# Projections of pool-conv and sparse attention as three fp32r products, attention outputs stored as halves

## The reference

```python
# second block, layer 0: pool-conv
proj = rms_norm(x, g) @ ab_w_in                    # 1024 x 1536: u_pool, u_val, u_gate
y = concat([pool_mixer(u_pool), conv_module(u_val, u_gate)]) @ ab_w_out   # 1024 x 1024
x = x + y
# second block, layer 1: sparse attention, 16 heads of 64
q, k, v, qi, ki, wi = split(rms_norm(x, g) @ c_w_in)
score = sum_h relu(qi_h . ki) * wi_h * scale       # 8 index heads; causal
sel = top_64(score)                                # keys kept for each query
x = x + softmax(q . k[sel] * 64**-0.5 + t5_bias) @ v[sel] @ c_w_out
# third block (twice): SwiGLU, then the hybrid mixer, then SwiGLU, each with a layer norm
y_ssm = mamba2(z, xbc, dt) @ w_ssm_out
y_att = moba_attention(q, k, v) @ w_att_out        # 8 heads of 128, one causal block of 256 keys
h = layer_norm(ALPHA * h + (g_ssm * y_ssm + g_att * y_att) @ w_o)
```

## Time and profile before

| | before |
|---|---|
| device time, median of 3 runs | 3935.52 us (3928.43 to 3944.9) |
| the profiled execution | 3925.62 us |
| its span | 3923.8 us |
| mean granted TensorE clock | 0.95 |
| TensorE busy | 3254.8 us (83%) |
| TensorE weight loads | 2228.5 us (57%) |
| VectorE busy | 2155.1 us (55%) |
| ScalarE busy | 1013.5 us (26%) |
| GpSimd busy | 1030.0 us (26%) |

### The profile page before, as it was taken

The page is one execution under the profiler, slowest core; times in us unless marked ns, Lnnn a source line. Parts: engine busy times, 40 slices in busy tenths (PEclk is TensorE's granted clock), DMA queues, the critical chain, the costliest instruction groups (busy, mean ns, idle before and its releaser), DMA issues. The chain is left out here.

```text
span 3923.8 us, 34661 instructions
## 1 busy us (share of the span) xinstructions
PE 3254.8 (83%) x12288; PEld 2228.5 (57%) x12288; DVE 2155.1 (55%) x3737; ACT 1013.5 (26%) x1593; POOL 1030.0 (26%) x1090
## 2 busy tenths in 40 slices
PE   5897577778987577777998999999998989978798
PEld 3663222223654222223877687876687868867686
DVE  5567766654547766654644445433455435555654
ACT  0212111111112111111432343411343422434333
POOL 0026777764015777775000000000000000200000
PEclk9799899999889899999999999999999989989999
DMA  9369999998539999998551455542355534243453
GB/s 364 142 260 385 409 409 409 409 399 328 212 123 380 409 409 409 409 409 326 172 185 65 140 185 168 189 150 97 119 192 166 190 130 143 76 157 122 150 183 118
DMA packets 402040, 951.18 MB, mean 242 GB/s; under 512 B 30652, under 2 KB 171488, under 8 KB 401632
## 3 DMA queue, kind: packets, MB, share of 16 engines
q0 software_dynamic: 147456, 536.94, 34.6%
q1 hardware_dynamic: 245088, 397.09, 29.7%
q10 hardware_dynamic: 9344, 15.22, 1.1%
HBM read 948.06 MB, written 1.07 MB: 242 GB/s over the span
## 5 line engine op out<-in xcount | busy, mean ns | idle before, releaser
L1451 PE MATMUL PS<-v_rows,xn 128*128 128x512 f32 x1944 | 910.0, 611 | 372.6 <-DMA v_rows<-in_peer_v_dram,peer_ids 369.7
L1451 PEld LDWEIGHTS PS<-v_rows,xn 128*128 128x128 f32 x1944 | 355.1, 193 | 926.4 <-issue 586.0
L1526 DVE CUSTOM_DVE_ANT_0 u_rows<-u_rows,PS 128x1024 f32<-128x1024 f32 x512 | 622.0, 1221 | 359.1 <-DMA u_rows<-in_peer_u_dram,peer_ids 331.4
L758 DVE TENSOR_TENSOR ring_lo<-ring,ring_hi 128x2048 fp32r<-128x2048 f32 x198 | 452.9, 2292 | 260.3 <-ACT ring_hi L697 259.8
L1590 POOL DMA_INDIRECT u_rows<-in_peer_u_dram,peer_ids x512 | 484.4, 946 | 282.2 <-issue 144.1
L1590 POOL DMA_INDIRECT v_rows<-in_peer_v_dram,peer_ids x512 | 486.0, 949 | 168.3 <-issue 143.0
L697 ACT CAST ring_hi<-ring 128x2048 fp32r<-128x2048 f32 x198 | 376.7, 1912 | 286.2 <-PE PS L614 156.2
L614 PE MATMUL PS<-ring_hi,hT_hi 128*128 128x512 f32 x1056 | 420.7, 398 | 16.6 <-DVE hT_lo L798 12.0
L614 PE MATMUL PS<-ring_hi,hT_lo 128*128 128x512 f32 x1056 | 414.8, 393 | 0.0
L614 PE MATMUL PS<-ring_lo,hT_hi 128*128 128x512 f32 x1056 | 414.0, 392 | 0.0
L440 PE MATMUL PS<-hT,ring 128*128 128x256 f32 x1664 | 364.0, 380 | 1.2 <-DVE hT L404 1.2
(11 more groups left out here) (395 smaller groups left out, 3714.4 us busy)
## 6 DMA issues: line engine op xcount, KB each, us to landing
ring<-in_ffn_w_gate_dram SPq DMA_DIRECT2D x132, 512.0 KB, 3.7
ring<-in_ffn_w_up_dram SPq DMA_DIRECT2D x132, 512.0 KB, 4.7
ring<-in_ffn_w_down_dram SPq DMA_DIRECT2D x66, 1024.0 KB, 4.9
ring<-in_w_in_dram SPq DMA_DIRECT2D x64, 1024.0 KB, 5.0
ada_ring<-in_ada_w_dram SPq DMA_DIRECT2D x96, 512.0 KB, 8.3
ring<-in_peer_wq_dram SPq DMA_DIRECT2D x16, 1024.0 KB, 5.4
ring<-in_c_w_in_dram SPq DMA_DIRECT2D x14, 1024.0 KB, 4.9
ring<-in_w_out_dram SPq DMA_DIRECT2D x8, 1024.0 KB, 11.4
```

The source lines that it names most:

```text
L758: nc.vector.tensor_tensor(halves(c)[1], slot, halves(c)[0], ALU.subtract).then_inc(S.w_lo, 1)
L1451: ins = nc.tensor.matmul(self.PS[:, 2 * b + h, :], diag[:, r % NDIAG, :], rowsV[:, m % VRING, h * BANK:(h + 1) * BANK], start=(n % (slots ...
L1526: ins = nc.vector.tensor_tensor_reduce(rowsU[:, m % URING, :], rowsU[:, m % URING, :], H[b], 1.0, 0.0, ALU.mult, ALU.add, dots[:, e:e + 1])
```

## The change

- `project_halves` makes every F product as three fp32r products of 256 columns (hi·hi, hi·lo, lo·hi), all into the same columns of a pair of banks; the four banks and the additions at emptying go. The T form is as it was, but in pairs of banks.
- `ab_in`, `ab_out`, `c_in` and `c_out` use it instead of `project`. Two helpers split the transposed tokens in two pieces each (`tokens_hi` on ScalarE, `tokens_lo` on VectorE). Chunks 2 and 3 of `c_in` (the index keys and weights) stay in plain fp32 and are left out of the halves (`plain`).
- `between` is called ahead of the wait for the root: VectorE makes the lo half of chunk 0 there.
- The pool and convolution stage makes the halves of its output and of the first chunks of `ab_out`.
- In both attentions the output leaves PSUM as two halves: ScalarE casts hi after the transposed probabilities of a later head, VectorE subtracts hi from the same PSUM tile. The split of all tokens in `att_out` goes.
- In `ssm_z` and `att_in` the queries and keys are emptied by ScalarE alone.

```diff
     def norm_vector(...):
+        if between:
+            between()
         ve.wait_ge(S.n_rstd, 1)
         for b in range(NB):
             nc.vector.tensor_scalar(self.xn[:, b, :], self.X[:, b, :], self.rstd[:, b:b + 1], None,
                                     ALU.mult).then_inc(S.n_xn, 1)
-        if between:
-            between()
...
+    def tokens_hi(self, act, S, hh):
+        act.drain()
+        for g in range(2):
+            if g == 1:
+                act.wait_ge(S.n_hT, self.N_HT)
+            self.nc.scalar.copy(hh[:, 4 * g:4 * g + 4, 0, :], self.hT[:, 4 * g:4 * g + 4, :]).then_inc(S.h_hi, 1)
+
+    def tokens_lo(self, ve, S, hh):
+        ve.drain()
+        for g in range(2):
+            ve.wait_ge(S.h_hi, g + 1)
+            self.nc.vector.tensor_tensor(hh[:, 4 * g:4 * g + 4, 1, :], self.hT[:, 4 * g:4 * g + 4, :], hh[:, 4 * g:4 * g + 4, 0, :],
+                                         ALU.subtract).then_inc(S.h_lo, 1)
...
     # project_halves, kind "F"
-                            out, col = self.PS[:, quad + t, :], slice(t * P, (t + 1) * P)
-                            nc.tensor.matmul(out, w_hi[:, kk, col], both[:, k, :], start=st, stop=False, skip_group_check=True)
-                            ins = nc.tensor.matmul(out[:, 0:SEQ], w_lo[:, kk, col], tok_hi[:, k, :], start=False, stop=sp,
-                                                   skip_group_check=True)
+                            out, col = self.PS[:, pair + t // 2, (t % 2) * SEQ:(t % 2 + 1) * SEQ], slice(t * P, (t + 1) * P)
+                            nc.tensor.matmul(out, w_hi[:, kk, col], tok_hi[:, k, :], start=(st and t % 2 == 0), stop=False, skip_group_check=True)
+                            nc.tensor.matmul(out, w_hi[:, kk, col], tok_lo[:, k, :], start=False, stop=False, skip_group_check=True)
+                            ins = nc.tensor.matmul(out, w_lo[:, kk, col], tok_hi[:, k, :], start=False, stop=sp, skip_group_check=True)
...
     # ab_in: TensorE, ScalarE, VectorE
-                    self.project(pe, S, [("F", 512)] * 3, self.hT, KT)
+                    self.project_halves(pe, S, ["F"] * 3, hh[:, :, 0, :], hh[:, :, 1, :], KT, ready=S.h_lo)
...
+                    self.weights_hi(act, S, 0, 2)
                     self.norm_scalar(act, S, gain, None)
+                    self.tokens_hi(act, S, hh)
+                    self.weights_hi(act, S, 2, 6)
...
+                    self.norm_vector(ve, S, gain, None, lambda: self.weights_lo(ve, S, 0, 1))
+                    self.tokens_lo(ve, S, hh)
+                    self.weights_lo(ve, S, 1, 2)
...
     # pool and convolution stage: ScalarE, then VectorE
+                    self.weights_hi(act, S, 0, 2)
+                    act.wait_ge(S.y_pool, 1)
+                    nc.scalar.copy(YT_hi[:, 0:4, :], YT[:, 0:4, :]).then_inc(S.y_hi, 1)
...
                         nc.scalar.activation(YT[:, 4 + c, :], conv[:, c, :], ACT.Silu, bias=b[:, c:c + 1], scale=g[:, c:c + 1])
+                    for c in (0, 2):
+                        if c == 0:
+                            nc.scalar.drain()
+                        nc.scalar.copy(YT_hi[:, 4 + c:6 + c, :], YT[:, 4 + c:6 + c, :]).then_inc(S.y_hi, 1)
...
                     nc.vector.tensor_tensor(sq[:], conv[:], conv[:], ALU.mult).then_inc(S.sq, 1)
+                    self.weights_lo(ve, S, 0, 1)
...
+                    for i, c in enumerate((slice(0, 4), slice(4, 6), slice(6, 8))):
+                        ve.wait_ge(S.y_hi, i + 1)
+                        nc.vector.tensor_tensor(YT_lo[:, c, :], YT[:, c, :], YT_hi[:, c, :], ALU.subtract)
+                        if i == 0:
+                            self.weights_lo(ve, S, 1, 2)
...
     # output_projection (ahead: chunks whose halves an earlier stage made)
-                self.project(pe, S, [("T", 512)] * 2, YT, KT)
+                self.project_halves(pe, S, ["T"] * 2, YT_hi, YT_lo, KT)
+                self.weights_hi(act, S, self.ahead, 4)
+                self.weights_lo(ve, S, self.ahead, 4)
...
     # attention
+            def out_lo(h):
+                ve.wait_ge(S.a_hi, h + 1)
+                nc.vector.tensor_tensor(YT_lo[rows(h), h // per, :], self.PS[rows(h), 4 + h % 2, 0:SEQ], YT_hi[rows(h), h // per, :],
+                                        ALU.subtract).then_inc(S.a_out, 1)
...
                 normalised(h)
                 if h >= 2:
-                    self.attention_out(ve, S, nc.vector.tensor_copy, h - 2, rows, per, YT)
+                    out_lo(h - 2)
...
+            def out_hi(h):
+                act.wait_ge(S.a_val, h + 1)
+                nc.scalar.copy(YT_hi[rows(h), h // per, :], self.PS[rows(h), 4 + h % 2, 0:SEQ]).then_inc(S.a_hi, 1)
...
                 turned(h)
+                if h >= 2:
+                    out_hi(h - 2)
+            for h in (heads - 2, heads - 1):
+                out_hi(h)
...
     # c_in: ScalarE
+                    self.weights_hi(act, S, 4, 8)
                     for h in range(8):
                         act.wait_ge(S.index, h + 1)
...
                     for j in (3, 5, 7):
+                        self.weights_hi(act, S, 2 * j + 2, 2 * j + 6 if j < 7 else 2 * j + 3)
...
     # c_in: VectorE
+                    self.weights_lo(ve, S, 4, 6)
                     self.leave(ve, 1)
...
+                    self.weights_lo(ve, S, 6, 8)
                     evacuate(2)
...
                         nc.vector.drain().then_inc(S.used, 1)
+                    self.weights_lo(ve, S, 8, 10)
...
     # att_out
-                    if i == 0:
-                        nc.scalar.copy(YT_hi[:], YT[:]).then_inc(S.y_hi, 1)
...
-                    if i == 0:
-                        ve.wait_ge(S.y_hi, 1)
-                        nc.vector.tensor_tensor(YT_lo[:], YT[:], YT_hi[:], ALU.subtract).then_inc(S.y_lo, 1)
```

More of the change, by code:

```diff
@@ L478, in project_halves @@
                 if n >= self.base + self.ahead:
-                    pe.wait_ge(S.w_lo, n - self.base - self.ahead + 1)
+                    pe.wait_ge(S.w_lo, self.halves_made(n))
+                if ready is not None and j == first:
+                    pe.wait_ge(ready, g + 1)
                 w_hi, w_lo = [ring[:, n % self.half_slots, :].rearrange("p (k n) -> p k n", k=4)
@@ L1784, in _, with output_projection, attention @@
                     nc.gpsimd.tensor_tensor(self.rstd[:], self.ms[:], self.neghalf[:, 0:NB], ALU.pow).then_inc(S.c_rstd, 1)
-            self.output_projection("ab_out", YT)
-    def output_projection(self, name, YT):
-        with self.stage("p_free0 p_free1", name) as (block, S):
+            self.output_projection("ab_out", YT_hi, YT_lo, 2)
+    def output_projection(self, name, YT_hi, YT_lo, ahead):
+        self.ahead = ahead
+        with self.stage("p_free0 p_free1 w_hi w_lo", name) as (block, S):
             @block.tensor
             def _(pe):
-                self.project(pe, S, [("T", 512)] * 2, YT, KT)
+                self.project_halves(pe, S, ["T"] * 2, YT_hi, YT_lo, KT)
+            @block.scalar
+            def _(act):
+                self.weights_hi(act, S, self.ahead, 4)
             @block.vector
             def _(ve):
+                self.weights_lo(ve, S, self.ahead, 4)
                 self.plain_residual(ve, S)
-    def attention(self, block, S, ctx, heads, dh, QT, KT_, V, mask, bias, YT):
+    def attention(self, block, S, ctx, heads, dh, QT, KT_, V, mask, bias, YT_hi, YT_lo):
         nc = self.nc
@@ L1938, in sparse_attention @@
             gain = self.col("mix_norm_2")[:, KT:2 * KT]
-            with self.stage("n_ms n_rstd n_xn n_tr n_hT p_free0 p_free1 rb rb_out index relu used", "c_in") as (block, S):
-                rel = self.sb("dsa_rel", [P, 2, W3], ctx=ctx)
-                sc = self.sb("dsa_scores", [P, W3], ctx=ctx)
-                top = self.sb("dsa_top", [P, NB, 8], ctx=ctx)
+            self.place_halves(ctx, 2)
+            self.plain = (2, 3)
+            with ExitStack() as inner, self.stage(
+                    "n_ms n_rstd n_xn n_tr n_hT p_free0 p_free1 w_hi w_lo h_hi h_lo rb rb_out index relu used", "c_in") as (block, S):
+                rel = self.sb("dsa_rel", [P, 2, W3], ctx=inner)
+                sc = self.sb("dsa_scores", [P, W3], ctx=inner)
+                top = self.sb("dsa_top", [P, NB, 8], ctx=inner)
+                hh = self.sb("dsa_tokens", [P, KT, 2, SEQ], F32R, ctx=inner)
+                halves = hh[:, :, 0, :], hh[:, :, 1, :], KT
                 @block.tensor
@@ L2070, in _ @@
                     pe.wait_ge(side, 48)
-                self.attention(block, S, ctx, AH, 64, QT, KT_, V, mask[:], B, YT)
-            self.output_projection("c_out", YT)
+                self.attention(block, S, ctx, AH, 64, QT, KT_, V, mask[:], B, YT_hi, YT_lo)
+            self.output_projection("c_out", YT_hi, YT_lo, 1)
     def turn_plain(self, pe, S, src):
@@ L2635, in _ @@
                 nc.vector.drain()
[L2636 to L2640 removed]
+                self.plain_residual(ve, S)
```

138 lines of the change are left out of this document (69 added, 69 removed).

## The result

The changed kernel takes 3953.45 us (median of 20 runs, 3939.52 to 3964.95), the kernel before 3937.98 us (20 runs, 3923.86 to 3944.9). The ratio is 1.0053, with a 95% interval of 1.0042 to 1.0065: 20.9 us slower by the ratio, between 16.5 and 25.6, and 15.5 by the two medians. The forecast was 3940 us, in a range of 3918 to 3960. One thing in the text ahead is wrong and changes no number: the third block runs once, not twice.

What follows compares the result with a forecast made beforehand. TensorE was taken as gapless in fp32 projections; in the attention loops VectorE and TensorE both repeat every 2.82 us. Stage terms summed to +0.1, the clock added +4: 3935.5 + 4.1 = 3940 us, range 3918 to 3960.

Steps and rivals of the forecast that it cites:

- clock term: Whole kernel: new waits make TensorE start at 1.2 GHz, about 2 us each; half of four starts, +4 us.
- rival (2): Attention loops: waits pull the clock down, making the loop TensorE-bound again; all 14 heads give 3960 us; chance 0.12.
- Products: Converted projections: three 256-wide fp32r products cost 0.348 us against 0.434 for fp32; three 512-wide ones 0.677 against 0.86.
- Rival (3): Projections: 256-wide products are bound by their weight loads, 0.57 us a triple, +85 us, 4025 us; chance 0.03.
- Loops: Both attention loops: VectorE waits for ScalarE's hi half, period 4.0 us; +16.5 us in sparse attention, +7.6 in the second.
- Rival (1): Attention loops: the hi-half wait isn't on the path, so 24.1 us go away, 3916 us; chance 0.09.
- The two stalls ahead of jobs 5 and 7: Sparse attention's input: ScalarE empties jobs 3 and 5 only after the fourth hi half; TensorE stands 3.1 us twice, +6.2.
- Start of `ab_in` and end of pool-conv: Pool-conv: first input product starts 2.95 us later; VectorE's extra halves at the end add 2.8 us.
- `c_out`: Sparse attention's output projection: cheaper 512-wide products save 5.8 us.
- Rival (4): Converted stages: ScalarE and VectorE make halves late at most chunks, 6 to 10 us in all, 3948 us; chance 0.11.
- `c_in`: Sparse attention's input stage: cheaper products against a later start, a longer index phase and two stalls, together -7.5 us.
- The removed split in `att_out`: Third block's output projection: dropping the split of all tokens in one piece removes TensorE's 2.26 us wait, -2.3 us.

Runs made afterwards that it cites:

- experiment 1: Changed kernel with ScalarE's hi cast of head h-2 moved ahead of the copy of head h's transposed probabilities; ratio to the kernel before 0.9979.
- experiment 3: Changed kernel with ScalarE, in the sparse input stage, emptying jobs 3 and 5 after the second hi half, not the fourth; ratio to the kernel before 1.0018.
- the repaired loop: Sparse attention's loop with the hi cast ahead of the transposed probabilities' copy, against the changed kernel's order; 50.2 to 58.7 us in six traces.
- The kernel with all repairs: Changed kernel plus earlier hi cast, both sparse-input reorderings, pool-conv's end over its output projection, chunk 0's lo half behind the scaling; 0.9877 and 0.9910 of the kernel before.

## Why the prediction held, and which step of it failed

**The range and the sign.** The measured 3953.45 us lie in 3918 to 3960. The forecast was no change to speak of, +4 us. By the ratio the change costs 20.9 us, just beyond the half per cent (0.53), a case that had a chance of 0.16; by the medians it is 15.5, within it. The mechanisms of the loops and the waits were right. That the range held is in part luck: its clock term was to lie between 0 and 8 us and came out at some 19, and the range reached 20 us above the forecast for the sake of rival (2), which came only in part.

**Products: right.** Forecast 0.348 us a triple, measured 0.354 and 0.360; over the 256 triples that replace fp32 products that is 2 us less gain. The 512-wide triples of `c_in` take 0.700 us, not 0.677, which is 0.7 more; those of `c_out` came out at 0.680. Rival (3) fell: with a load for each product the spacing is 0.12, and not the 0.19 of a load. The rule of the Trainium skill that was weighed ("TensorE: Matmul & The Clock Gate", Part 3, what overlaps and what doesn't: loads overlap running products only when their row groups differ) is not what this trace shows, where all loads use all rows.

**Loops: right.** Forecast were a period of 4.0 us, 16.5 and 7.6 us more; measured 3.9 and 4.2 in turn, and against the first trace before 12 to 21 us and 9 to 9.6 us more (five traces). The chain was the one that was written down, instruction by instruction, and experiment 1 takes it away with a change of order alone. Rival (1) fell with that.

**The two stalls ahead of jobs 5 and 7: right**, 3.03 us for a forecast of 3.1. The index phase went to 9.2 us (2618.16 to 2627.32), forecast 8.3.

**Start of `ab_in` and end of pool-conv: right**, +3.15 for +2.95 (from the end of the last SwiGLU product to the first of `ab_in`, 2054.50 to 2065.20 before, 2047.93 to 2061.78 after) and +2.45 for +2.8 (TensorE's wait ahead of `ab_out`, 3.72 and 6.17). **`c_out`: right**, -5.7 for -5.8 in the first trace; in the second, where the clock was low at its start, -3.5. Rival (4) fell: no wait for `weights_lo` stands in a steady run of a stage that the change converts.

**The step that failed: the clock.** "I count half of four such starts: +4. The cost lies between 0 and 8." Against the same products at the full clock, the low clock costs the first trace 2.8 us in `ab_in`, 1.0 more than before in `ab_out`, some 6 in `c_in`, 1.7 in `att_out` and 2.9 in `mix3_out`. The loops are 2.8 and 2.0 us over their forecast, which counted none; that this is the clock as well is inferred, not measured apart. Together that is 19 us, in the second trace several less (`mix3_out` 1.6 less, the sparse loop 5.1). `c_in` shows it best: forecast -7.5, measured +2.4, though the start and both stalls came out to 0.2 us. Of the 9.9 us that were missed some 6 are the clock, 1.7 the price of the triples and 0.9 the index phase; the rest is not accounted for. The four starts that the prediction counted are the first products of two stages, the index phase and the second attention's loop, at half a start each. The two stalls that it had itself priced at 3.1 us each were not among them, and behind each the clock was low: experiment 3 got back 3.6 us of clock with the two. TensorE behind the wait ahead of job 5, and in the second attention's loop, which answers to the last of the earlier trace rows:

```profile
2654.00:2658.00 4.00, 3.08 (x14) 3.08 (x15) 3.93 (x5) 0.87 (x2) 0.00 (x0) 0.63 0.58 222
...
3592.00:3627.00 35.00, 24.12 (x88) 19.01 (x88) 17.70 (x56) 14.75 (x49) 0.00 (x0) 0.65 0.00 0
```

The loop's mean clock went from 0.82 to 0.65. In this stage idle time and low clock came together: the low clock is part of the price of the wait.

**Rival (2)** came in part. In the first trace the clock fell again in the middle of the sparse loop, for 7 us (and a third time in its last heads):

```profile
2723.00:2730.00 7.00, 7.00 (x22) 4.32 (x22) 2.33 (x8) 2.60 (x9) 0.00 (x0) 0.52 0.00 0
```

Not for all 14 heads: the loop took 68.6 to 77.4 us in the five traces that have this order, around the 72.7 of the forecast.

**Terms at nothing.** `mix3_out` and `att_in` had no term of their own in the forecast. `ssm_out` and `att_in` are together 1.2 to 1.5 us longer, most of it in the key jobs (25.04 us before, 25.96 after). The removed split in `att_out` (2.26 us of wait) brought 0.2 to 0.6, not 2.3, because the clock was low for the first 3.5 to 4.2 us of the stage. In the traces with the repaired loop it is not low there, and the stage takes 69.6 us: the forecast's 2.3 are there.

## What to carry to other kernels

When a copy is split in two between engines, the second engine's wait must be placed by when the first engine comes to its part in its own list, not by when the data is there: here one line moved up made 22 to 29 us. Cheaper products leave more idle time on TensorE, and in this kernel each new wait of some 3 us had to be charged with its own length and a start at the low clock, 1.5 to 3 us. A step of a few microseconds is read from its stage, in two traces of each kernel; the whole time can't show it.

## What the runs showed that was not expected

The granted clock stood at either level in the same stage behind the same wait, and the same way in both traces of each kernel: the sparse attention's loop took 57.1 and 50.2 us in two kernels that are the same there, and in another trace of each 58.7 and 50.2. A stage that no change touched took 134.2 and 138.0 us in two executions of one kernel. And a reordering that was made for 1.5 us in each of two norms gave 12 us by the medians, 7 of them in that loop. The kernel with all repairs ran at 0.9877 and 0.9910 of the kernel before on two occasions, faster than both kernels.
